# A decoder trunk on one core: entries of the RWKV and gated delta stages, gate logarithms, first RWKV chunk and attention's end, rearranged

## The reference

```python
def macaron_half(x, g, w_gate, w_up, w_down):
    h = rmsnorm(x, g)
    return x + 0.5 * ((jax.nn.silu(h @ w_gate) * (h @ w_up)) @ w_down)

def rwkv7_mix(u, shift_prev, S0, p, v_first, vres):      # u = rmsnorm(x)
    prev = jnp.concatenate([shift_prev[:, None, :], u[:, :-1]], axis=1)
    xx = prev - u
    xr, xw, xk = u + xx * mu[0], u + xx * mu[1], u + xx * mu[2]
    xv, xa, xg = u + xx * mu[3], u + xx * mu[4], u + xx * mu[5]
    r, k, v = xr @ w_rkv[0], xk @ w_rkv[1], xv @ w_rkv[2]
    wlog = -jax.nn.softplus(-(w0 + jnp.tanh(xw @ w1) @ w2)) - 0.5     # w1: 1024 x 64
    a = jax.nn.sigmoid(a0 + (xa @ a1) @ a2)                            # a1: 1024 x 64
    gate = jax.nn.sigmoid(xg @ g1) @ g2                                # g1: 1024 x 160
    ...                     # a recurrence over positions, in chunks of 64; w_o

def gdn_mix(u, conv_prev, S0, p):
    proj = u @ p['w_in']                      # q, k, v, z and 16 gate columns b, a
    xp = jnp.concatenate([conv_prev, qkv], axis=1)
    conv = sum(p['conv_w'][j] * xp[:, j:j + T] for j in range(4))
    beta = jax.nn.sigmoid(b_raw)
    g = -jnp.exp(p['a_log']) * jax.nn.softplus(a_raw + p['dt_bias'])
    ...                     # delta rule in chunks of 64; gated norm; w_o
```

## Time and profile before

| | us |
|---|---|
| median of 3 runs | 2826.32 (2824.7 to 2826.5) |
| the profiled execution's own time | 2830.97 |
| its span | 2829.3 |
| PE busy | 2769.8 (98% of the span) |
| DVE, ACT, POOL busy | 1688.9 (60%), 1237.5 (44%), 281.3 (10%) |

### The profile page before, as it was taken

How to read it: one execution, slowest core, us unless ns; L and a number is a source line. 1 busy time by engine, 2 the same in 40 slices (tenths; PEclk the granted TensorE clock), 3 DMA queues, 4 the chain that set the end, 5 groups by cost and what they waited for, 6 DMA issues and landing times.

```text
span 2829.3 us, 60521 instructions
## 1 busy us (share of the span) xinstructions
PE 2769.8 (98%) x26549; PEld 2597.0 (92%) x26549; DVE 1688.9 (60%) x2581; ACT 1237.5 (44%) x1958; POOL 281.3 (10%) x343
## 2 busy tenths in 40 slices
PE   9999999999999999999999999999999999999999
PEld 8997978999999986999999888789999978798999
DVE  5646865665565456665564584546556558766653
ACT  5434643544443334444443563234444336444443
POOL 2001023000000211000000111410000010121000
PEclk9999999999999999999999999999999999999999
DMA  9443401644644754444543433255465343205542
GB/s 280 140 147 121 136 33 36 199 149 143 195 152 143 251 187 160 149 159 148 183 159 124 153 124 121 56 166 165 132 191 168 129 145 137 61 4 168 164 132 78
DMA packets 351610, 402.49 MB, mean 142 GB/s; under 512 B 31290, under 2 KB 306127, under 8 KB 350989
## 3 DMA queue, kind: packets, MB, share of 16 engines
q1 hardware_dynamic: 340448, 361.76, 40.0%
q0 software_dynamic: 10976, 38.07, 4.4%
HBM read 385.22 MB, written 14.57 MB: 141 GB/s over the span
## 4 chain that ended last, share of the span: by engine, by line
PE 89%; DVE 6%; ACT 3%; issue 1%; DMA 1%; POOL 0%; SPq 0%; DVEq 0%; ACTq 0%; POOLq 0%
PE banks L1016 24%; PE banks L1018 23%; PE banks L1017 23%; PE banks L1431 1%; PE banks L1404 1%; PE banks L1138 1%; PE banks L1006 1%; PE banks L1602 1%; PE banks L1012 1%; PE banks L1555 1%; PE banks L1914 1%; DVE work L2882 0%; DVE ring_lo L2906 0%; PE banks L1379 0%; PE banks L1348 0%
## 5 line engine op out<-in xcount | busy, mean ns | idle before, releaser
L2831 DVE TENSOR_TENSOR w_lo<-ring,w_hi 128x2048 fp32r<-128x2048 f32 (+1 forms) x303 | 609.0, 2010 | 410.3 <-ACT w_hi L2288 410.1
L1016 PE MATMUL banks<-h_hi,w_hi 128*128 128x288 f32 x2816 | 836.9, 297 | 1.3 <-DVE h_lo L2823 0.8
L1017 PE MATMUL banks<-h_hi,w_lo 128*128 128x288 f32 x2816 | 831.4, 295 | 0.0
L1018 PE MATMUL banks<-h_lo,w_hi 128*128 128x288 f32 x2816 | 828.5, 294 | 0.0
L2288 ACT CAST w_hi<-ring 128x2048 fp32r<-128x2048 f32 (+1 forms) x303 | 510.5, 1685 | 572.7 <-PE banks L1018 543.9
L1016 PEld LDWEIGHTS banks<-h_hi,w_hi 128*128 128x128 f32 x2816 | 528.2, 188 | 3.7 <-DVE h_lo L2823 1.9
L1018 PEld LDWEIGHTS banks<-h_lo,w_hi 128*128 128x128 f32 x2816 | 531.0, 189 | 0.0
L1017 PEld LDWEIGHTS banks<-h_hi,w_lo 128*128 128x128 f32 x2816 | 529.3, 188 | 0.4
L1016 PE MATMUL banks<-hid_hi,w_hi 128*128 128x288 f32 x1408 | 416.1, 296 | 0.0
L1017 PE MATMUL banks<-hid_hi,w_lo 128*128 128x288 f32 x1408 | 415.4, 295 | 0.0
L1018 PE MATMUL banks<-hid_lo,w_hi 128*128 128x288 f32 x1408 | 414.3, 294 | 0.0
(11 more groups left out here) (614 smaller groups left out, 4311.7 us busy)
## 6 DMA issues: line engine op xcount, KB each, us to landing
ring<-in_ffn_w_gate SPq DMA_DIRECT2D x87, 1024.0 KB, 5.5
ring<-in_ffn_w_up SPq DMA_DIRECT2D x87, 1024.0 KB, 8.0
ring<-in_ffn_w_down SPq DMA_DIRECT2D x64, 768.0 KB, 4.6
ring<-in_ffn_w_down SPq DMA_DIRECT2D x64, 640.0 KB, 5.8
ring<-in_rwkv_w_rkv SPq DMA_DIRECT2D x24, 1024.0 KB, 6.4
ring<-in_gdn_w_in SPq DMA_DIRECT2D x16, 1024.0 KB, 7.4
ring<-in_attn_w_qkv SPq DMA_DIRECT2D x12, 1024.0 KB, 7.3
ring<-in_rwkv_w_o SPq DMA_DIRECT2D x8, 1024.0 KB, 6.3
```

Source lines behind the costliest of these rows:

```text
L1016: nc.tensor.matmul(out, w_hi_k, x_hi_k, start=start, stop=False)
L1017: nc.tensor.matmul(out, w_lo_k, x_hi_k, start=False, stop=False)
L1018: return nc.tensor.matmul(out, w_hi_k, x_lo_k, start=False, stop=stop)
L2831: nc.vector.tensor_tensor(w_lo[e][:, 0:k, :], raw, w_hi[e][:, 0:k, :], ALU.subtract).then_inc(w_lo_ready, 1)
```

## The change

Seven edits in five places.

1. RWKV entry (both RWKV stages): the decay and the rate mix are no longer made. `(u + xx*mu) @ w` is taken as `u @ w + xx @ (mu*w)`. ACT scales the two weight blocks by their rates into `shift_w` (16 instructions of 128 x 64), which lies in `W(XM1_)`. PE runs one pass over `h` and one over `W(XX_)`, with the two 64-wide products of a tile side by side. DVE writes all eight tiles of `h` first, then the sample columns of `xx` in two instructions for all tiles, then the last columns, and has 16 mixes fewer. `keep_clock(5, 5)` becomes `keep_clock(5, 3)`. The transposes for the shift output come behind both passes and wait for nothing more.
2. First RWKV chunk (both stages): `keep_clock(5, 2)` and the transposes of the first sample state come ahead of level 1; the other three states move to levels 1 to 3, and level 4 has none. ACT and DVE copy out accordingly.
3. Attention's end: `keep_clock(.., 3)` behind the sample output's transposes.
4. Gated delta entry: the convolution rows lie elsewhere, so that POOL can fetch them three units earlier, ahead of its sums of squares for this entry; 12 of the 24 transposes stand ahead of `norm`, 12 behind, with one `keep_clock` product; DVE copies them out behind `h`, and ACT's first copy of `h` waits for them.
5. Gate logarithms: taken at piece 0 with the table that `norm` left, the sigmoid at piece 2; DVE makes the low part of piece 3 between, ahead of its convolution of piece 0.

```diff
@@ PE, rwkv @@
-                keep_clock(5, 5)
-                p = 0
+                keep_clock(5, 3)
                 unit_in(b)
                 wa = ring[:, b % SLOTS, :]
-                for i, (off, width, at) in enumerate(((0, 64, HALVES[0]), (512, 64, HALVES[1]), (1024, 160, slice(0, 128)))):
-                    src = W((XM0_, XM1_, XM0_)[i])
-                    for k in range(CH):
-                        after(xm_ready)
-                        last = nc.tensor.matmul(bank[p][at, 0:NT], w[:, k, 0:min(width, 128)], src[:, k, :],
-                                                start=(k == 0), stop=(k == CH - 1))
...
+                for k in range(CH):
+                    pe.wait_ge(h_ready, 8 * normed_before[s] + k + 1)
+                    for i, at in enumerate(HALVES):
+                        nc.tensor.matmul(bank[i][at, 0:NT], wa[:, 512 * i + 64 * k:512 * i + 64 * k + 64], h[:, k, :],
+                                         start=(k == 0), stop=False)
+                after(last_cols_ready)
+                pe.wait_ge(xx_first, 2 * j + 2)
+                for k in range(CH):
+                    pe.wait_ge(xx_ready, CH * j + k + 1)
+                    for i, at in enumerate(HALVES):
+                        last = nc.tensor.matmul(bank[i][at, 0:NT], shift_w[:, i, k, :], W(XX_)[:, k, :], start=False, stop=(k == CH - 1))
...
@@ PE, first chunk @@
-                    if c == 0 and l < 5:
...
+                    if c == 0 and l < 4:
+                        after(seq_t_ready_act)
+                        after(seq_t_ready_dve)
+                        sample_transposes(l, old)
...
+                    else:
+                        pe.wait_ge(matnt_raw, 2 * NCHUNK * j + 1)
+                        keep_clock(5, 2)
+                        pe.wait_ge(s0_in, 16 + 128 * (j + 1))
+                        sample_transposes(0, old)
                     chunk_inverse(c, meanwhile, behind)
@@ PE, attention @@
                 last.then_inc(sample_raw, 1)
+                keep_clock(OUT_SPREAD_BANK[0], 3)
                 after(ao_ready)
                 head_norms(Q_, 0, OUT_SPREAD_BANK)
@@ PE, gdn @@
                 after(conv_in, 16)
-                for c in range(24):
...
+                conv_columns(0)
                 norm(s)
-                keep_clock(5, 2)
+                conv_columns(12).then_inc(prev_raw, 1)
+                keep_clock(5, 1)
@@ ACT, rwkv @@
                 b = unit_base[s]
+                act.wait_ge(slot_full[b % SLOTS], full(b))
+                for i, m in enumerate((1, 4)):
+                    for k in range(CH):
+                        nc.scalar.activation(shift_w[:, i, k, :], ring[:, b % SLOTS, 512 * i + 64 * k:512 * i + 64 * k + 64],
+                                             ACT.Copy, scale=prm[:, mu:mu + 1])
@@ ACT, gdn: gate_logs, once at c == 3, now at c == 0 @@
-                    log_table()
                     after(g_abs)
...
-                    nc.scalar.activation(gcol[:, BETA], graw[:, 0], ACT.Sigmoid).then_inc(g_ln, 1)
...
+                    if c == 2:
+                        nc.scalar.activation(gcol[:, BETA], graw[:, 0], ACT.Sigmoid)
@@ DVE, rwkv @@
-                for c in range(4):
+                for c in range(CH):
                     normed(c, NORM + 8 * (3 * (3 * j) + 1))
...
+                sample_shift()
...
-                for i, m in enumerate((1, 4, 5, 3, 0, 2)):
+                for i, m in ((2, 5), (3, 3), (4, 0), (5, 2)):
@@ POOL @@
-                pool.wait_ge(half_done, HD(unit_base[s] - 1, 1))
+                pool.wait_ge(half_done, HD(unit_base[s] - 4, 1))
                 pool.dma_start(conv_rows, t["state_gdn_conv"][0].rearrange("b j n -> (b j) n")).then_inc(conv_in, 16)
```

More of the change, by code:

```diff
@@ L1114, in rwkv @@
+                last.then_inc(last_rows_transposed, 1)
+                p = 2
+                w = wa[:, 1024:1024 + 8 * 160].rearrange("p (k n) -> p k n", n=160)
+                for k in range(CH):
+                    after(xm_ready)
+                    last = nc.tensor.matmul(bank[p][:, 0:NT], w[:, k, 0:128], W(XM0_)[:, k, :], start=(k == 0), stop=(k == CH - 1))
+                last.then_inc(half_done, 1)
+                p += 1
                 gate_tail = wa[:, 1024:1024 + 8 * 160].rearrange("p (k n) -> p k n", n=160)[:, :, 128:160]
@@ L1734, in gdn, with conv_columns @@
                 base = proj_before[s]
+                def conv_columns(c0):
+                    for c in range(c0, c0 + 12):
+                        last = nc.tensor.transpose(bank[1 + c // 12][:, 24 * (c % 12):24 * (c % 12) + 24],
+                                                   conv_rows[:, 128 * c:128 * c + 128], ident[0:24, 0:24])
+                    return last
                 after(conv_in, 16)
[L1736 to L1739 removed]
+                conv_columns(0)
                 norm(s)
[L1741 removed]
+                conv_columns(12).then_inc(prev_raw, 1)
+                keep_clock(5, 1)
                 unit_in(b)
@@ L2623, in gate_logs @@
                     act.wait_ge(act_step, 6)
[L2624 to L2625 removed]
+                    nc.scalar.activation(gtmp[:, 0], gtmp[:, 0], ACT.Ln, bias=ones[:, 0:1]).then_inc(g_ln, 1)
                 def convolved(c):
@@ L3083, in rwkv @@
                             chunk_output(c - 1, l - 2)
+                        if c == 0 and l == 1:
+                            turned_states(0)
                         if c == 0 and l <= NCHUNK:
@@ L3325, in gdn @@
                 after(prev_raw)
-                for i in range(2):
-                    last = V.tensor_copy(conv_prev[:, 12 * i:12 * i + 12, :].rearrange("p c n -> p (c n)"), bank[1 + i][:, 0:288])
-                last.then_inc(prev_ready, 1)
                 inverse_rms(s)
@@ L3335, in gdn @@
                     TT(h_lo[:, c, :], h[:, c, :], h_hi[:, c, :], ALU.subtract).then_inc(split_lo, 1)
+                for i in range(2):
+                    last = V.tensor_copy(conv_prev[:, 12 * i:12 * i + 12, :].rearrange("p c n -> p (c n)"), bank[1 + i][:, 0:288])
+                last.then_inc(prev_ready, 1)
                 for i in range(4):
```

97 lines of the change are left out of this document (41 added, 56 removed).

## The result

The changed kernel takes 2803.55 us in the median of its first 4 runs (2803.15 to 2807.93), where the kernel before took 2825.51 in 4 runs beside it: a ratio of 0.9917, 95% interval 0.9905 to 0.9929. In a later set it was 2804.44 (5 runs) against 2829.27 (15 runs), 0.9911 (0.9896 to 0.9926). So 22.0 us were gained in the one, 24.8 in the other; 26.5 had been forecast. The two profiled executions, 2830.97 and 2803.15, lie 27.8 apart.

A forecast was written before the change was run, and what follows sets the result against it. PE, busy 98%, was taken as the bound. RWKV entries 10.0, first chunks 6.5, attention's end 0, gated delta entry 6.0 and gate sums 4.0 make 26.5 us: 2799.8 from the median, range 2794 to 2811.

The forecast's parts named there:

- what bounds the kernel: Whole span: PE, busy 98%, alone sets the end, so gains must cut its pauses, its work or its half-clock stretches.
- a gain is the same from either: Whole span: the 26.5 us summed on the profiled execution (2830.97) was also subtracted from the median of runs (2826.32).
- At half clock half the time is lost: First RWKV chunks: without a pause the clock should not fall, winning 1.5 us in the first stage, 2.6 in the second.
- the six of before: Six low-clock stretches, 21 us together, behind pauses at RWKV first chunks, attention's end, gated delta entry, gate sums, second RWKV entry.
- (1): Pauses filled with transposes: the lower clock stays or comes elsewhere, costing about 7 us, total 2807 (2804 to 2811); chance 0.17.
- The trace agrees at this place: Gated delta entry: clock at 0.50 from 1586 to 1590 despite busy PE, read as transposes not counting as busy.
- (2): The clock holds but one term gives half, likely the entry's DVE chain or gates' low parts: 2803 to 2808; chance 0.09.
- (3): RWKV entries: the two 64-wide products don't run side by side, 1.01 us a step, total 2814; chance 0.05.
- (5): RWKV entries: switching column halves makes PE wait for the running product, up to 2.4 us a step, total 2860; chance 0.04.
- (4): The gain is handed back at the next wait, above all for weights: 2821 to 2832; chance 0.04.
- Edits costed at nothing: RWKV entry: ACT's 16 weight scalings, at most 6.9 us, covered before the second pass; PE's 16 extra half-width products fill waits.
- the term of 0: Attention's end: three filling products make it 1.6 us later, full clock 1.6 shorter; bounds 0.3 won to 1.6 lost.

The follow-up runs named there:

- run 10: Not a number: "another run", then "10 us". That run is the changed kernel with the first RWKV chunks as before; median 2813.34 us.

## Why the prediction came out as it did

**Right: what bounds the kernel, and each term.** No term between the profiles is off by more than 0.4 (table above), and the total is 27.5 where 26.5 was said. The details hold too: passes of 4.25 and 4.10, level 1 of the first chunk 0.6 later (0.8 said), level 2 earlier by 1.5 and 2.65 (1.4 and 2.6 said), no wait at the gate sums, none for the convolution rows.

**Off: the base of the sum.** The forecast was 2800.0, the result 2803.55. The step that failed is the sentence "a gain is the same from either". The sum was made on the profiled execution, where it gives 2804.5, and then taken from a median 4.65 lower (2825.51 in the comparison itself). Of the gain 11.8 us were stretches at half clock; they belong to the execution in which they were seen, and a run of before that has fewer of them is lighter and has less to win. The line through the 26 runs says the same: at a clock of 1.000, which is beyond all runs, before would take 2821.3 (2.5 to either side), 18 above after, near the 15.7 of the table that aren't clock. With the ordinary median of before, 2829.3, the sum gives 2802.8. The start that stays low longer, 1.5 in after's second profile, would cover most of what is left to 2804.4, but whether the runs of before have it too isn't known.

**Right by a wrong price.** "At half clock half the time is lost" held closely for the instructions named (1.5 said and measured in the first stage, 2.6 said and 2.9 measured in the second). For a stretch as a whole it doesn't: 0.36 per us at the gated delta entry, and 0.38 over the six of before, which last 30.7 us in the clock's records, not the 21 of the windows in the earlier trace rows, for 11.8 lost. The products of the projection start 0.24 apart at half clock and 0.13 apart at full, which makes 0.45 us for each us filled with them alone.

**Rivals.** (1), the clock stays low where fills are transposes: out, by the 27 transposes that stand where leaving them out lets the clock fall. "The trace agrees at this place" was a wrong reading, since the clock had fallen ahead of the transposes. Its weaker form, low stretches elsewhere, is real but seldom: 2 of 9 runs, 4 us. (2): no term gave half; DVE beside POOL did stretch the chain, by 0.5 over the forecast, seen in the second pass ending 12.5 and not 12 behind the sum, and 1.3 a stage could be had back. (3) and (5): a step is 0.51, and undoing the order costs 9.3. (4): PE's list of waits has none for a transfer of weights in either kernel.

**Edits costed at nothing.** Right for ACT's scalings (L2323, 3.92 for 16, forecast at most 6.9, done by 2289.7 and first needed at 2293.3) and for the filling in the first chunks. For attention's end the term of 0 was the balance of 1.6 won by the clock and 1.45 spent on filling; three executions without the fill (the second one of before among them) kept their clock there, so in such a run the edit loses 1.45.

## What to carry over

When a gain includes stretches at a lower clock, keep those terms apart and take the sum from the execution in which they were seen; collect the clock of some twenty runs before believing a median of three. A pause is filled for the clock's sake where removing the fill has been shown to cost: here one product of 0.9 us was worth 6.4, three others cost 1.45, and the rest did nothing that a run could show. Applying a linear mix to weights instead of data turns eight steps of another engine into products that can start at once, and the two halves then want to be issued in turn, column half by column half.

## What the runs showed of the hardware that I had not expected

- A 64-column fp32 product over 288 columns costs 0.49 us alone (records 0.24 apart, two to a product), and a pair in turn on the two halves of the array 0.51. Where eight on one half were followed by eight on the other, up to four records ran side by side at the change.
- fp32 transposes held the granted clock as products do at the one place where leaving out the fill costs time (7 in place of one product of 0.9 us: five runs of 2803.7 to 2806.5, against 2810.3 to 2811.4 without).
- A pause of 0.94 us was followed by 17 us at half clock in a fully busy PE (all five runs were longer by 6), and in another run 10 us at half clock came with no pause over 0.06 us ahead of them, while pauses of 0.4 to 1.5 at the RWKV entry, and of 1.08 at attention's end, passed in some executions with 1.00 and in others not.
- DVE's tile of h (three operands, 128x288) took 0.71 with POOL subtracting beside it and 0.53 with POOL away from the first five; DVE's mixes took 0.44 alone and 0.49 with POOL beside the first of them.
- A start at half clock can be missing from the clock's records: in three profiles they begin at 17 to 18 us and windows ahead of that print 1.00, while products start 0.24 apart there and 0.13 apart behind.
